# Holding back one weight load of stage C until the last probabilities are in DRAM

## The reference, cut to what matters

```
h = x @ w_in[l] + b_in[l]
q, k, v, z_a, u_g, v_g, z_g, g_a, g_g = split_columns(h)
y_a = sliding_window_attention(q, k, v, attn_sinks[l]) * silu(z_a)
y_g = chunked_spatial_gating(gelu(u_g), gelu(v_g), ...) * silu(z_g)
br_a = y_a @ w_branch_attn[l]
br_g = y_g @ w_branch_gmlp[l]
merged = sigmoid(g_a) * br_a + sigmoid(g_g) * br_g
out = merged @ w_out[l] + b_out[l]
x = layer_norm(ALPHA * x + out, ln_g[l], ln_b[l])
```

## Time and profile before

| | us |
|---|---|
| median of 3 runs | 1539.45 |
| lowest and highest run | 1538.2, 1539.75 |
| span of the profiled execution | 1541.3 |
| PE busy in it | 1526.5 |
| DVE, ACT, POOL busy | 1045.9, 577.6, 360.1 |

### The profile page before, as it was taken

How to read it: one execution, slowest core, us unless ns; L and a number is a source line. 1 busy time by engine, 2 the same in 40 slices (tenths; PEclk the granted TensorE clock), 3 DMA queues, 4 the chain that set the end, 5 groups by cost and what they waited for, 6 DMA issues and landing times.

```text
span 1541.3 us, 29779 instructions
## 1 busy us (share of the span) xinstructions
PE 1526.5 (99%) x12343; PEld 1368.3 (89%) x12343; DVE 1045.9 (68%) x1750; ACT 577.6 (37%) x1038; POOL 360.1 (23%) x333
## 2 busy tenths in 40 slices
PE   9999999999999999999999999998999999999998
PEld 9999999999998899899898898887888988888887
DVE  6656565775867678676887678777615787787346
ACT  5323222353354244434445455472112256541121
POOL 0000000020422124032342124334430043343510
PEclk9999999999999999999999999999999999999999
DMA  5322322323333334323334143554234334562331
GB/s 171 110 83 84 104 88 83 110 82 103 98 115 91 103 102 119 111 84 101 94 112 148 60 136 96 164 159 128 84 108 137 98 114 148 148 169 82 121 125 55
DMA packets 151859, 170.75 MB, mean 111 GB/s; under 512 B 6348, under 2 KB 122480, under 8 KB 151728
## 3 DMA queue, kind: packets, MB, share of 16 engines
q1 hardware_dynamic: 119728, 138.71, 29.4%
q10 hardware_dynamic: 31920, 29.97, 6.6%
q0 software_dynamic: 80, 0.20, 0.0%
HBM read 151.82 MB, written 17.04 MB: 110 GB/s over the span
## 4 chain that ended last, share of the span: by engine, by line
PE 48%; DMA 2%; DVE 1%; issue 0%; ACTq 0%; ACT 0%
PE acc L415 13%; PE acc L417 13%; PE acc L416 13%; PE aux L417 1%; PE aux L416 1%; PE aux L415 1%; PE aux L1420 1%; DMA p_turn<-sqs 1%; DMA pt_second<-p_turn 1%; PE aux L1463 1%; DMA p_turn<-xns 1%; PE aux L1438 1%; PE aux L1439 0%; PE aux L1386 0%; PE aux L643 0%; PE aux L645 0%
## 5 line engine op out<-in xcount | busy, mean ns | idle before, releaser
L415 PE MATMUL acc<-xhis,whi 128*128 128x264 f32 (+2 forms) x1848 | 609.0, 330 | 0.0
L417 PE MATMUL acc<-xhis,wlo 128*128 128x264 f32 (+2 forms) x1848 | 601.9, 326 | 0.0
L416 PE MATMUL acc<-xlos,whi 128*128 128x264 f32 (+2 forms) x1848 | 601.8, 326 | 0.0
L415 PEld LDWEIGHTS acc<-xhis,whi 128*128 128x128 f32 x1848 | 348.1, 188 | 29.5 <-issue 0.6
L417 PEld LDWEIGHTS acc<-xhis,wlo 128*128 128x128 f32 x1848 | 347.9, 188 | 29.2
L416 PEld LDWEIGHTS acc<-xlos,whi 128*128 128x128 f32 x1848 | 348.2, 188 | 27.1
L410 POOL TENSOR_TENSOR wlo<-raw,whi 128x1024 fp32r<-128x1024 f32 x84 | 206.7, 2462 | 371.9 <-DVE whi L2612 371.9
L406 ACT ACTIVATE whi<-raw 128x1024 fp32r<-128x1024 f32 x158 | 164.0, 1048 | 131.5 <-PE acc L417 119.3
L410 DVE TENSOR_TENSOR wlo<-raw,whi 128x1024 fp32r<-128x1024 f32 x81 | 99.8, 1235 | 36.9 <-ACT whi L406 36.7
L2290 DVE TENSOR_TENSOR wlo<-raw,whi 128x1024 fp32r<-128x1024 f32 x77 | 95.0, 1236 | 27.3 <-ACT whi L406 27.1
L2612 DVE CAST whi<-raw 128x1024 fp32r<-128x1024 f32 x84 | 61.4, 733 | 54.0 <-PE acc L417 53.8
(11 more groups left out here) (394 smaller groups left out, 2781.1 us busy)
## 6 DMA issues: line engine op xcount, KB each, us to landing
raw<-in_w_in SPq DMA_DIRECT2D x38, 1024.0 KB, 5.6
raw<-in_hgrn_w_in SPq DMA_DIRECT2D x32, 1024.0 KB, 5.9
raw<-in_pool_w_in SPq DMA_DIRECT2D x15, 1024.0 KB, 5.6
raw<-in_pool_w_out SPq DMA_DIRECT2D x8, 1024.0 KB, 5.0
raw<-in_hgrn_w_out SPq DMA_DIRECT2D x8, 1024.0 KB, 5.1
raw<-in_w_out SPq DMA_DIRECT2D x8, 1024.0 KB, 5.0
v_turn<-vb ACTq DMA_DIRECT2D x8, 544.0 KB, 2.7
raw<-in_pool_w_grp SPq DMA_DIRECT2D x4, 1024.0 KB, 5.1
```

The costliest lines, as they stand in the source:

```text
L415: pe.matmul(dst, stat[0], mov[0], start=first, stop=False)
L416: pe.matmul(dst, stat[0], mov[1], start=False, stop=False)
L417: return pe.matmul(dst, stat[1], mov[0], start=False, stop=last)
```

## The change

SP gets one more wait in each layer. Before the chunk with gg2 and gg3 it waits until `pb_sent` of attention step 15 of that layer has counted, which is when the last probabilities have landed in DRAM. `GG_SECOND` is the number of that chunk in the layer.

```diff
--- before.py
+++ after.py
@@ -886,6 +886,7 @@
             return order
 
         C_ORDER = c_slots()
+        GG_SECOND = next(m // 2 for stage, index, kind, m, half, u in C_PLAN if (stage, index) == ("gg", 2))
 
 
         def freed_c(M):
@@ -1048,6 +1049,9 @@
                         chunks.append(("vg", w_out_c[:, 8 * i + 4 * c:8 * i + 4 * c + 4, 512 * j:512 * j + 512]))
                 for n, (kind, src) in enumerate(chunks):
                     N = C_PIECES // 2 * i + n
+                    if n == GG_SECOND:
+                        last = len(ATT) * (i + 1) - 1
+                        sp.wait_ge(pb_sent[last % 3], 16 * (last // 3) + 16)
                     if n == len(chunks) - 2:
                         sp.wait_ge(yalo_ready, 4 * i + 4)
                         sp.wait_ge(yglo_ready, 4 * i + 4)
```

## The result

The changed kernel takes 1544.87 us, the median of 14 runs (1543.75 to 1548.11), beside 1539.64 (1536.88 to 1544.82, 14 runs) for the kernel before. The ratio is 1.0026, interval 1.0017 to 1.0035: slower by 4 us (the two medians lie 5.2 us apart), where 4 us less was forecast. The profiled execution took 1545.8 us with a span of 1544.0. So 1.8 us lie around the span, and the execution of before that the prediction worked from took about 1543.1, above its median.

The account below looks back on a forecast made before the run. PE was taken to bound the kernel, losing time at line 1420's read-back wait. Savings of 4.1 us wait and 1.5 us clock (first layer) and 0.1 us (second) made 5.7 us; forecast 1535.4 us, range 1533.4 to 1540.2.

Parts of the forecast that it names:

- What bounds the kernel: PE, busy 1526.5 of 1541.3 us; in stage C it waits at line 1420 for read-back probabilities, 4.5 and 0.5 us.
- Point 1 of the sum: Without the load in front, step 15's write to DRAM lands 5.5 us after issue, bounds 5.4 and 9.36 us.
- a spread write needs no protection: If the probability write ran on 16 engines instead of 4, the change would bring nothing.
- Point 2: ACT's first read-back follows the sigmoid of ga3, at about 1051.8 in place of 1053.81: 2.0 us earlier in the first layer.
- Point 3: Held load and read-backs overlap about a microsecond, sharing engines without loss; last landing 1056.9, leaving 0.4 us wait per layer.
- Point 4: Bra's load behind the last read-back decides 5.79 or 2.79 us; the change gives a lead of 2.05 us.
- Point 5: The late chunk makes DVE stand at worst 2.2 us for piece 28 and costs nothing in PE's time.
- The clock: PE's slower clock after the first layer's long wait costs 1.5 us, which a short wait would save.
- the first rival: The held load falls on the read-backs; second layer loses up to 4.0 + 1.5 us: 1545 us; chance 0.15.
- The second: Rival: the wait before line 1420 is mostly gone in timed runs; 1538.5 to 1539.2 us, no change; chance 0.20.
- The third: Rival: the write takes 8 to 9 us without the load too; no first-layer gain, mostly no change; chance 0.10.
- the signs that the prediction named for being wrong: Write still over 7 us, last read-back over 4 us, or line 1420 of the second layer waiting longer than before.

Follow-up runs that it names:

- the four-part write: The kernel before, no load held, with each layer's last probability write cut into four DMAs of 32 partitions: 1536.72 us, ratio 0.9973.
- the run with the fast, protected write: The changed kernel, SP's wait kept, with the last write cut into four DMAs: 1539.3 us, ratio 0.9989 against the kernel before.
- the runs where it was gone: Against the changed kernel, load held until ACT issued the last read-back (1545.66 us, ratio 1.0028) or until the read-backs landed (1549.79 us, 1.0045).
- the repeat: The changed kernel profiled once more, no edit: 1545.21 us.

## Why the prediction was wrong

*What bounds the kernel* was right: PE, and in stage C this one wait with its clock. The error of it was to take one execution for the rule. The two layers weren't a bad one and a good one; each draws anew. That also made the gain in reach too large, since the profiled execution was an unlucky draw, 3.5 us above the median of the runs (1543.1 and 1539.64).

*Point 1 of the sum is the step that failed first.* It put the write at 5.5 us, between 5.4 and 9.36. It takes 7.15 and 7.20 us after the change, 7.1 and 7.3 with the change in one layer. So the load was worth 2.2 us of the first layer's 9.36 and 1.2 us of the second's 8.40, not 3.9 and 2.9. The likely reason is that the term was taken from a write that stood alone: the row of 5.4 us has no other transfer of ACT's queue issued within 5 us before or behind it. At 1044 to 1045, when step 15's write is issued, ACT's queue is still at work on earlier transfers, on a quarter of the engines:

```profile
q10 hardware_dynamic: 51, 0.10, 26.8%
```

The prediction had named this as the bound's reason and took the nearest row all the same. That few engines are a large part of it is shown by the four-part write (3.3 us). The read-backs of steps 12 and 13, issued from 1046.31 on, flow beside the write: from 1046.5 to 1051.5 the queue moves 0.70 MB, and the write is 0.26 MB:

```profile
q10 hardware_dynamic: 1066, 0.70, 51.4%
```

How the rest divides between them and the write of step 14 stays open: no run took either away. The write of step 14 stood in front of the four-part write too, and that one landed after 3.3 us.

The Trainium skill (DMA: Bandwidth & Descriptors, "Why a DMA increments its semaphore by 16 and not by 1") gives a DMA the largest number of engines, up to 16, that divides the slowest dimension of both its sides: 4 for the whole write, 16 for each part of 32 partitions. The trace agrees with the first in its 26.8% of 16 engines. That the parts use more is shown by the run with the fast, protected write, where ACT's queue had 54.7% from 1045 to 1046; that it is all 16 isn't shown. The prediction's sentence that a spread write needs no protection held, and the held kernel with it shows that protection then costs.

*Point 2*, the read-backs tied to the sigmoid of ga3, was right (0.09 us behind it). It is also what made the collision certain. The write lands at 1051.91 and the sigmoid starts at 1051.90, so both queues are let go together; in all six held layers SP's issue and the first read-back are within 0.12 us. With a landing at 1049.9 the load would have had 2 us of lead.

*Point 3 failed too, and not only with point 1.* It had the queues share without loss. The load's data and the read-backs' flow together, and the load gets far more: 74.9% against 27.7%, then 106.0% against 4.5%. The last read-back takes 5.6 to 6.3 us in both layers, not 3.8, and a wait of 2.9 us stays on PE's weight loads, not 0.4. A write as fast as point 1 had it would not have saved the forecast: in the held kernel with the four-part write it landed after 3.3 us, the load had a lead of 4 us, and the last read-back still took 5.16 and 4.20 us.

*Point 4* was right, as the kernel with bra's chunk held shows (2.72 us), but it wasn't the term that the change worked on, and the race hangs on less than its 1 us: 0.29 us of lead and less lose. A lead over bra's load of 2.1 us (1055.56 - 1053.48) helps nothing when another load is nearer.

*Point 5* held for this change: DVE stood for 1.2 to 1.3 us (at worst 2.2 was forecast), and PE didn't notice, for the reason that it gave: what follows on DVE waits for PE's line 1424 in any case, 4.32 us in the first layer. That reason goes when PE's wait goes. In the runs where it was gone, DVE's 3.7 and 5.1 us cost at least what the collision had (ratios 1.0028 and 1.0045 beside 1.0026).

*The clock* went as the first rival had it in the first profile, 0.50 behind the wait in both layers; in the repeat the second layer kept 1.00.

*The rivals.* The first, that the held load falls on the read-backs, is what happened, by its own mark (a landing 7 us or more after the issue) and near its price: 1545 was worked out, 1544.87 measured. That the number fits so well is luck. It had nothing or 1 to 2 us of gain in the first layer and up to 5.5 us of loss in the second; the sections show 1.6 us of gain and 3.6 of loss against the profiled execution, and most of the rest of the 5.2 us between the medians is that this execution was 3.5 us slower than its median. It had 0.15. The second was half right: the long wait is in part of the runs. The third is refuted in its strong form, since the write takes 7.2 us and not 8 to 9. All three of the signs that the prediction named for being wrong came: a write over 7 us, a last read-back over 4, and a longer wait in the second layer.

## What to carry to other kernels

When a transfer is held back until another has landed, ask who else waits for that same landing: here both started at once, and the large load got most of the engines' time. A transfer that uses few engines may gain more by its shape than by a clear road in front of it: 3.3 us against 7.2 us here. Before a load is made late, look at what the engine that needs it would do meanwhile in a run without the loss. And where two queues race, read the chain in both repeats of the stage and in more than one execution before pricing either: a narrow spread of the sections, not one good value, shows that a race is settled.

## What the runs showed of the hardware

- Two queues don't share the engines by halves. While a load of 1 MB ran, the read-backs had 27.7% beside its 74.9%, then 4.5% beside its 106.0%, and once it was through they had 116.5%. The Trainium skill (the same page, "Queues, rings and completion order") says that an engine takes turns between queues, a packet at a time. The trace has packets of about 1 KB on one side (0.49 MB in 483) and 0.5 KB on the other (0.13 MB in 249). If these are the packets of that rule, which no run shows, turns would give the read-backs a third of the data. They had a quarter of it for 1.5 us (0.13 beside 0.39 MB) and a twenty-fifth for the next (0.02 beside 0.49 MB): the measurement decides. Why isn't shown.
- The same wait does or doesn't cost PE its clock. Waits of 2.43 and 2.51 us (PE's own, with the change) were followed by a granted clock of 0.50, 1.2 GHz; waits of 2.67 us (held in the first layer) and 3.54 us (the change, repeated, second layer) left the 28 matmuls at full speed, 1.75 us, as here in the stretch behind that last one:

```profile
1384.00:1386.00 2.00, 2.00 (x31) 1.83 (x25) 0.85 (x2) 0.12 (x1) 0.48 (x1) 1.00 0.29 107
```

A price for the clock from one row, as the prediction's 1.5 us, is therefore a draw as well.
